# Operands of a projection made inside the projection's own stage, and eight of the first layer's modulation rows moved from the setup to VectorE during the first projection

## The reference, cut to what matters

```python
# first block, for layer 0 and layer 1
shx, scx, gtx = adaln_params(c, adaln_w[layer], adaln_b[layer])        # 3 x 1024 rows: shift, scale, gate
shc, scc, gtc = adaln_params(c_ctx, adaln_w[layer], adaln_b[layer])
hx = rms_norm(x, norm_g[layer]) * (1.0 + scx[:, None, :]) + shx[:, None, :]
hc = rms_norm(ctx, norm_g[layer]) * (1.0 + scc) + shc
ox, oc = mixer(hx, hc, ...)          # begins with a wide projection of hx and hc
x = x + gtx[:, None, :] * (ox @ w_out[layer])
ctx = ctx + gtc * (oc @ w_out[layer])
# second block
h = concatenate([meta, x])
u = rms_norm_2(h, norm1_g)
p = u @ w_in                          # 43 tiles of 128 output rows
...
merged = g[:, :, 0] * ya + g[:, :, 1] * yb + g[:, :, 2] * yc
h = h + merged @ w_o
h = h + hier_moe(rms_norm_2(h, norm2_g), ...)
```

## Time and profile before

| | |
|---|---|
| median of 3 runs | 3600.99 us |
| the profiled execution itself | 3605.53 us |
| its span in the trace | 3603.7 us |
| PE busy | 2956.3 us (82%) |
| DVE busy | 1624.4 us (45%) |
| ACT busy | 1231.2 us (34%) |
| POOL busy | 159.5 us (4%) |

### The profile page before, as it was taken

One profiled execution on the slowest core, in us unless ns is written; L12 is line 12 of the kernel. 1 busy time (PEld: TensorE's weight loads), 2 busy tenths in 40 slices (PEclk: granted clock), 3 DMA queues, 4 the chain that ended last, 5 costly groups with the idle time before them and its releaser, 6 DMA issues. The chain is left out here.

```text
span 3603.7 us, 36460 instructions
## 1 busy us (share of the span) xinstructions
PE 2956.3 (82%) x14078; PEld 2306.6 (64%) x14078; DVE 1624.4 (45%) x2616; ACT 1231.2 (34%) x1972; POOL 159.5 (4%) x258
## 2 busy tenths in 40 slices
PE   7799997957775979996894889999897378748883
PEld 2577885636664758883663679988665267637773
DVE  1566335637774130005553235431243453357786
ACT  2444212435553131113432221111143211237776
POOL 0000000100000000000000000000000020020002
PEclk9899998979997979996897989999999699769997
DMA  5223333253303013221214013333332641269996
GB/s 221 88 105 134 135 122 87 72 155 98 81 8 107 18 53 132 85 70 66 79 36 165 23 60 122 114 102 97 95 97 54 251 133 59 90 238 357 371 384 253
DMA packets 144304, 452.02 MB, mean 125 GB/s; under 512 B 18258, under 2 KB 39378, under 8 KB 142836
## 3 DMA queue, kind: packets, MB, share of 16 engines
q1 hardware_dynamic: 100196, 280.78, 23.1%
q0 software_dynamic: 27520, 98.02, 7.9%
q10 hardware_dynamic: 16416, 70.90, 5.4%
HBM read 322.68 MB, written 126.95 MB: 125 GB/s over the span
## 5 line engine op out<-in xcount | busy, mean ns | idle before, releaser
L948 PE MATMUL acc<-act_hi,w_hi 128*128 128x512 f32 (+3 forms) x2512 | 704.5, 378 | 204.0 <-PEq L967 110.2
L948 PE MATMUL acc<-act_lo,w_hi 128*128 128x512 f32 (+3 forms) x2512 | 685.2, 370 | 0.0
L948 PE MATMUL acc<-act_hi,w_lo 128*128 128x512 f32 (+3 forms) x2512 | 683.5, 370 | 0.0
L948 PEld LDWEIGHTS acc<-act_hi,w_hi 128*128 128x128 f32 x2512 | 449.8, 191 | 300.3 <-issue 220.8
L730 DVE TENSOR_TENSOR w_lo<-w_stage,w_hi 128x1024 fp32r<-128x1024 f32 x114 | 139.7, 1225 | 921.8 <-ACT w_hi L616 921.8
L948 PEld LDWEIGHTS acc<-act_lo,w_hi 128*128 128x128 f32 x2512 | 447.1, 191 | 80.2
L948 PEld LDWEIGHTS acc<-act_hi,w_lo 128*128 128x128 f32 x2512 | 445.5, 190 | 78.7
L616 ACT ACTIVATE w_hi<-w_stage 128x1024 fp32r<-128x1024 f32 x114 | 120.9, 1060 | 1073.2 <-PE acc L948 1073.2
L2670 DVE TENSOR_TENSOR expert_lo<-expert_stage,expert_hi 128x1024 fp32r<-128x1024 f32 x186 | 225.9, 1223 | 80.6 <-ACT expert_hi L2613 78.1
L2613 ACT ACTIVATE expert_hi<-expert_stage 128x1024 fp32r<-128x1024 f32 x186 | 195.8, 1058 | 91.7 <-DMA expert_stage<-in_exp_w 46.4
L1722 DVE TENSOR_REDUCE max<-scores 128x1 f32<-128x256 f32 (+6 forms) x256 | 117.2, 484 | 148.9 <-PE scores L1846 148.0
(11 more groups left out here) (360 smaller groups left out, 4236.8 us busy)
## 6 DMA issues: line engine op xcount, KB each, us to landing
expert_stage<-in_exp_w SPq DMA_DIRECT2D x186, 512.0 KB, 6.5
w_stage<-in_w_in SPq DMA_DIRECT2D x43, 512.0 KB, 4.3
rope<-out_stage ACTq DMA_DIRECT2D x26, 640.0 KB, 3.6
proj<-out_stage ACTq DMA_DIRECT2D x26, 640.0 KB, 5.3
slots_in<-zero SPq DMA_DIRECT2D x1, 15872.0 KB, 42.3
residual<-slots_in POOLq DMA_DIRECT2D x31, 512.0 KB, 7.3
slots_out<-residual POOLq DMA_DIRECT2D x31, 512.0 KB, 6.7
w_stage<-in_ab_w_in SPq DMA_DIRECT2D x26, 512.0 KB, 5.0
```

Source lines behind the costliest of these rows:

```text
L948: mmi = eng.matmul(a[:, t, 0:n], lhs[:, j.w % 2, kb:kb + P], rhs[:, c0 + k, off:off + n], start=first, stop=last)
```

## The change

There is no norm stage and no split stage any more. Their work is inside the projection that follows:

- **Feed.** A `Feed` lists the pieces (tile, k) of the operand. DVE scales piece `i + 2` (`normalized`) while ACT rounds piece `i + 1` (`operand_high`) and DVE subtracts piece `i` (`operand_low`); or SP loads the piece from DRAM (`load_operand`), and ACT and DVE split it. A ring of 4 buffers (6 for the output projections) is between them.
- **Lead.** The first two jobs are done tile by tile (`lead = 2`): job 0's first token tile, job 1's first, job 0's second, and so on, and each matmul waits for its own piece only. In the last `gemm_phase` `lead` is 0; its pieces are 256 tokens wide.
- **Squares.** The sums of squares of the residual are made where the residual is made: in the setup (ACT squares, DVE adds) and in the two output projections (`squares`, `add_squares`). One matmul of ones per tile is left at a projection's start.
- **Weights.** The first two weight tiles are split one at a time among the first pieces, no longer at the end of the stage before.
- **Setup.** `adaln_w` is loaded without its gate third and after the residual; 8 × 4 matmuls in place of 8 × 6, 16 transposes in place of 24.
- **Gates.** The 8 gate rows of the first layer are made by DVE in the first projection, ahead of the second layer's 24: one row per `rope` job and two per `store` job from job 5 on. POOL loads their weights.
- **Order.** The first projection's second job is now tile 5 (a `store` job), which was 14th.
- **Restore.** Before the second output projection the residual comes back in four DMAs on POOL's queue while the projection runs.

Core of the diff:

```diff
-            modulated(0, hi, lo, wts)
+            order = [0, 5, *range(1, 5), *range(10, 18), *range(18, 22), *range(6, 10), *range(22, 26)]
...
+            for i in range(KD):                       # setup, ACT
+                eng.wait_ge(x_in[i], 32)
+                if i >= 3:
+                    eng.wait_ge(summed, i - 2)
+                eng.activation(E.sums[:] if i == 0 else sq[:, i % 2, :], E.X[:, i, :], ACT.Square).then_inc(sq_ready, 1)
...
-                for g in range(6):
+                for g in range(4):
...
+            if feed.norm is not None:                 # projection, DVE
+                normalized(0)
+                normalized(1)
+            split_w(0)
+            for i in range(len(feed.pieces)):
+                operand_low(i)
+                if feed.norm is not None and i + 2 < len(feed.pieces):
+                    normalized(i + 2)
+                if i == 1:
+                    split_w(1)
+            eng.wait_ge(fed_lo, len(feed.pieces))
...
+            for t in range(len(jobs[0].tiles) if lead else 0):      # projection, TensorE
+                for i in range(lead):
+                    if t == 0:
+                        eng.wait_ge(w_lo, jobs[i].w + 1)
+                    products(i, [t])
...
+                            if hi is feed.hi and feed.number.get((c0 + k, off), 0) > fed[0]:
+                                fed[0] = feed.number[c0 + k, off]
+                                eng.wait_ge(fed_lo, fed[0])
...
+            if restore is not None:                   # projection, POOL
+                for i in range(KD // 2):
+                    eng.dma_start(E.X[:, 2 * i:2 * i + 2, 0:META + T], restore[:, 2 * i:2 * i + 2, :]).then_inc(restored[i], 16)
...
-                    modulate(i - 5)
+                    for f in itertools.islice(mods, 1 if j.kind == "rope" else 2):
+                        modulate(f)
```

More of the change, by code:

```diff
@@ L929, in rope_aux, with products @@
                            start=True, stop=True).then_inc(aux_done, 1)
-            for i, j in enumerate(jobs):
-                a = acc[i % 2]
-                if j.w >= 2:
-                    eng.wait_ge(w_lo, j.w - 1)
-                if i >= 2:
-                    eng.wait_ge(free[i % 2], free_before[i])
-                if j.a.merged:
-                    eng.wait_ge(m_lo, 2 * KD)
-                if j.kind == "down":
-                    eng.wait_ge(he_lo, j.a.needs)
+            fed = [0]
+            def products(i, tiles):
+                j, a = jobs[i], acc[i % 2]
                 hi, lo, c0 = j.rhs
@@ L951, in _ @@
                                 mmi.then_inc(mm, 1)
-                    if k % 2 == 1 and pending:
+                    if i >= lead and k % 2 == 1 and pending:
                         rope_aux(*pending.pop(0))
-                while pending:
-                    rope_aux(*pending.pop(0))
+            if feed.norm is not None:
+                for t, (off, n) in enumerate(feed.tiles):
+                    eng.matmul(acc[1][:, t, 0:n], col(E.con, CONST_AT, "ones"), feed.norm.sums_of(off, n),
+                               start=True, stop=True).then_inc(ss_done, 1)
@@ new lines, in _ @@
+            for t in range(len(jobs[0].tiles) if lead else 0):
[3 more added lines that the diff above has]
+                    products(i, [t])
+            for i, j in enumerate(jobs):
+                if i >= lead:
+                    eng.wait_ge(w_lo, j.w + 1)
+                    if i >= 2:
+                        eng.wait_ge(free[i % 2], free_before[i])
+                    if j.a.merged:
+                        eng.wait_ge(m_lo, 2 * KD)
+                    products(i, range(len(j.tiles)))
+                    while pending:
+                        rope_aux(*pending.pop(0))
@@ L2955, in qblocks @@
             return [(P * b, P) for b in bl] + ctxb, masks
+        first.close()
         def head(r, a):
@@ L3006, in build @@
             wts = Weights(nc, c, [d["w_in"][f] for f in order])
[L3007 to L3008 removed]
+            norm = Norm(lambda k, off, n: E.X[:, k, off:off + n], lambda off, n: E.sums[:, off:off + n],
+                        lambda k, t: par("norm1", k), lambda k, t: None)
+            feed = Feed([(t, k, *tile) for t, tile in enumerate(TILES2) for k in range(KD)], hi, lo, 2, 4, norm=norm, tiles=TILES2)
             jobs = []
```

497 lines of the change are left out of this document (224 added, 273 removed).

## The result

The changed kernel takes 3462.28 us, the median of 4 runs (3455.53 to 3472.18), against 3600.88 us (3598.75 to 3604.33, 4 runs) for the kernel before: ratio 0.9616, 95% interval 0.9591 to 0.9642. The forecast was 3443 us in 3426 to 3490. The profiled execution took 3459.37 us against 3605.53 before. So 146.2 us are gone there, where the sum had 157.9.

A forecast was written before the change was run, and what follows sets the result against it. TensorE bounds the projections; DVE, ACT or a DMA bound the six norm and split stages, 223 us together. Gains sum to 157.9 us: 3605.5 to 3447.6 profiled, less 4.5 to the median, forecast 3443 us, range 3426 to 3490.

The forecast's parts named there:

- Norm stages: Three dissolved stages ahead of projections: pieces made under the first two jobs' products, gaining 40.4, 40.9 and 32.5 us.
- Split stage 1: Dissolved stage ahead of the first output projection: TensorE is the bound from the first product at about 7; gain 16.3 us.
- 2.6 at the lower clock: Split stage 1: 2.6 us added to the new start for TensorE running at the lower clock.
- Split stage 2: Second layer's output projection: residual and pieces share the DMAs, 9.5 MB in 24 us at 400 GB/s; gain 20.2 us.
- Setup: Before the first projection: 64 row records instead of 96, rows done at 53.3 us; gain 7 us.
- the first chunk lands at about 24 instead of 15: Setup: first weight chunk later, behind small loads and half the residual in SP's queue; at 27, the setup gains 4 us.
- Gates: First projection: DVE's 8 more rows, 20 us of work, cost nothing; without cover at most 20 us.
- Narrow products: 256-wide products in the leads: 0.133 us each; with weight loads' 0.169 as floor, 3.4 us more.
- B: Rival: clock stays at 0.50 for the lead in all five fed starts, costing 89 us, 3532 us; chance 0.06.
- C: Rival: norm-stage pieces made in turn without overlap, 2.2 us each, +14, +18 and +11 us, 3486 us; chance 0.06.
- D: Rival: interrupted start leaves the clock at 0.50 for the whole first projection, about 3860 us; chance 0.02.
- E: Rival: job 0 waits for the last piece after all, so little overlap, about 3530 us; chance 0.03.

The follow-up runs named there:

- experiment 6: Changed kernel plus idle multiplications before the first product, two per norm stage and four in the first two split stages; 3457.27 us, ratio 0.9615 to the kernel before.
- Experiment 5: Changed kernel, but POOL issues the residual's way back in the second layer's output projection only after the first eight pieces; 3452.32 us, ratio 0.9590 to the kernel before.
- Experiment 4: Changed kernel with other setup orders: modulation weights ahead of the residual, 3453.41 us; chunks shared 5 to 3 with row copies between the squares, 3448.77 us.
- experiment 3: Changed kernel with layer 0's eight gate rows made in the setup again, not on VectorE in the first projection; 3471.22 us, ratio 0.9649 to the kernel before.

## Why the prediction was right, point by point

- *Norm stages (forecast 113.8, measured 114.1).* Right in each step, here for the first, with S the start of the stage: the first product at S + 6.8 (6.6), the pieces 1.32 us apart, the rounding of tile 2 at S + 37.4 with job 2 running at S + 41.4 (43.3). The errors are 1 to 2 us, and that they cancel to 0.3 is luck. The first lost 2 us in a stall at job 3, which I had not seen: with two jobs ended at once, job 0's roots, whose sums are made during job 2, stand on ACT ahead of weight tile 3. The forecast had named such a handover for job 2 only.
- *Split stage 1 (16.3, 16.3).* Right in size. The term "2.6 at the lower clock" was wrong in kind: in experiment 6 the full clock gave back about 1 us. By the same windows TensorE then waits for pieces (busy 4.58 of 6 us); that their loads are the rest is argued, not shown.
- *Split stage 2 (20.2, measured 12.9).* The step that failed is "they share the DMAs with the pieces ... the first tile's products at 18.5". Job 0's products of the first tile ended at S + 25.5. The DMAs moved 337 to 348 GB/s in the stage's first 26 us and not 400, and the order was wrong: the residual's transfers came at once and took their part from the start, when nothing else can hide the wait. Experiment 5 shows 9.6 us.
- *Setup (+7, measured −0.6).* The failed step is "the first chunk lands at about 24 instead of 15". It landed at 31.4, past the worst case I had allowed for (27). I had shared the 430 GB/s by bytes ahead in SP's queue, as if SP got half. Experiment 4 shows that the order is the cause: with the weights first it landed at 17.9.
- *Gates (0).* Right for the first projection, and shown by experiment 3. The reciprocal's stall moved and kept its size, as said: 7.2 us.
- *Narrow products.* At the end of the first lead, at clock 1.00, they start 0.12 us apart:

```profile
103.13 0.28 PE L950 MATMUL acc<-act_hi,w_lo 128*128 128x256 f32 x1
103.25 0.28 PE L950 MATMUL acc<-act_hi,w_hi 128*128 128x256 f32 x1
```

  So the weight loads' 0.169 us are no floor, and the forecast's 0.133 was a little high.

- *Rivals.* B: the clock was 0.50 for 6 to 9 us after the first product in four starts, and for 18 us in split stage 2, where TensorE waited longest; then it rose to 1.00. Waits between the bursts can hold it at 0.50, as B feared (in experiment 6 they brought it back there), but it stayed there for a part of the lead only, and mostly in time that TensorE would have waited. C: the pace was 1.32 and not 2.2. D: 0.98 over the first projection. E: the run that builds it took 3562; the 3530 that I had put on it was too low.

The two missed terms are 15 us, small errors and the untouched stages gave 3 back: 12 us in the profiled executions (3459.4 against 3447.6). The upper end of the range, 3490, had been set by rival C and not by these two steps. The rest of the 19 us between 3443 and 3462 is how each profiled execution lies to its median, 4.5 us over it before and 2.9 under it after.

## What to carry to other kernels

When a preparing stage is dissolved into the stage that uses its result, price the new start piece by piece: the first piece's arrival, the slower of the two engines' pace per piece, and the handover to the first job outside the lead. In the three norm stages and the first split stage those sums came out within 2 us. What came out wrong was each place where transfers that had been ordered by a barrier were set free: there, write down which queue each one stands on and what else is issued at that moment, and hold back by a wait whatever isn't needed first. And do not price a low clock in full on an engine that waits for its operands: here the full clock gave back about 1 us where 2.6 had been priced.

## What the runs showed of the hardware

- An issue of a DMA is not free on a compute engine. With 1 MiB weight chunks at the head of its queue, ACT's eleventh to thirteenth issue took 2.8 to 4.3 us in place of 0.5 to 0.7, and an activation behind them started at 18.28 us, against 6.23 once it stood ahead of them. In the changed kernel, with the smaller residual ahead, ACT's twelve issues took 0.5 us each in the mean. What limit is met isn't shown.
- A reciprocal of 128x2048 float32 on VectorE takes 12.95 us, while an addition of a constant to the same tile takes 1.22. Cut in parts of 700 and 880 columns it took 4.53 and 5.65 us.
- In split stage 1 TensorE had clock 1.00 at its first product when idle multiplications had filled 6.2 us ahead of it, and without them only 5.8 us of products later. In the norm stages and split stage 2, where it then waited between the pieces, the clock fell back to 0.50 after about 5 us.
- The expert block, untouched, took 402.7 to 415.4 us in the fourteen traces, with granted clocks of 0.92 to 0.89.
